# A product of the identity with ones between the down and the up projections of a fp32 feed-forward on Trainium2

## What is computed

```python
FFN_HIDDEN = -(-8 * D_MODEL // (3 * 256)) * 256      # 5632
...
        hf = modulate(rms_norm(x, norm_ffn_gain[l]), sh_f, sc_f)
        gate_h, up_h = jnp.split(hf @ w_ffn_in[l], 2, axis=-1)
        x = x + g_f[:, None, :] * ((jax.nn.silu(gate_h) * up_h) @ w_ffn_out[l])
```

## Time and profile before

| | us |
|---|---|
| median of three runs | 2655.31 (2654.34 to 2657.0) |
| the profiled execution, its own time | 2652.7 |
| its span, first to last instruction | 2650.9 |
| TensorE busy | 2518.7 (95%) |
| GpSimdE busy | 1002.0 (38%) |
| VectorE busy | 912.5 (34%) |
| ScalarE busy | 787.6 (30%) |

### The profile page before, as it was taken

The page is one execution under the profiler, slowest core; times in us unless marked ns, Lnnn a source line. Parts: engine busy times, 40 slices in busy tenths (PEclk is TensorE's granted clock), DMA queues, the critical chain, the costliest instruction groups (busy, mean ns, idle before and its releaser), DMA issues.

```text
span 2650.9 us, 33839 instructions
## 1 busy us (share of the span) xinstructions
PE 2518.7 (95%) x11449; PEld 2036.6 (77%) x11449; DVE 912.5 (34%) x1487; ACT 787.6 (30%) x1490; POOL 1002.0 (38%) x764
## 2 busy tenths in 40 slices
PE   5589999999799999989999999999999999999999
PEld 3577777887677778768888888888888888888887
DVE  4755332157766666675201020202020201010112
ACT  2023224232455542232222222222222222222221
POOL 0024333444200024434444444444444444444443
PEclk8579999999788899989999999999999999999999
DMA  8732122365212246645222222222222222222223
GB/s 307 256 133 80 64 90 88 107 235 192 87 62 68 79 160 223 213 151 183 96 96 95 93 90 94 95 95 95 91 91 95 95 95 94 89 94 95 95 95 111
DMA packets 86204, 315.74 MB, mean 119 GB/s; under 512 B 9584, under 2 KB 10240, under 8 KB 84736
## 3 DMA queue, kind: packets, MB, share of 16 engines
q1 hardware_dynamic: 84240, 303.31, 34.1%
q10 hardware_dynamic: 1904, 11.62, 1.2%
HBM read 310.69 MB, written 4.19 MB: 119 GB/s over the span
## 4 chain that ended last, share of the span: by engine, by line
PE 59%; issue 29%; POOL 10%; DVE 2%; POOLq 0%; ACT 0%; DVEq 0%; ACTq 0%
PE ps L366 55%; POOL wlo L318 10%; PE ps L643 1%; PE ps L672 1%; PE ps L661 1%; DVE macc L1111 1%; PE ps L650 0%; POOLq L317 0%; DVE nsq L1361 0%; DVE biasT L1387 0%; PE ps L678 0%; PE ps L628 0%; POOL kn L340 0%; PE ps L632 0%; DVE rq L1364 0%
## 5 line engine op out<-in xcount | busy, mean ns | idle before, releaser
L318 POOL TENSOR_TENSOR wlo<-raw,whi 128x512 fp32r<-128x512 f32 x728 | 963.5, 1324 | 1481.4 <-ACT whi L800 1222.4
L800 ACT ACTIVATE whi<-raw 128x512 fp32r<-128x512 f32 x612 | 386.5, 632 | 1241.7 <-PE ps L366 1239.1
L366 PE MATMUL ps<-hfH,whi 128*128 128x512 f32 x1408 | 559.3, 397 | 12.3 <-DVE hfL L1493 11.5
L366 PE MATMUL ps<-hfL,whi 128*128 128x512 f32 x1408 | 558.7, 397 | 0.0
L366 PE MATMUL ps<-hfH,wlo 128*128 128x512 f32 x1408 | 558.1, 396 | 0.0
L366 PEld LDWEIGHTS ps<-hfH,whi 128*128 128x128 f32 x1408 | 266.1, 189 | 75.8 <-issue 12.3
L366 PEld LDWEIGHTS ps<-hfH,wlo 128*128 128x128 f32 x1408 | 266.2, 189 | 61.9
L366 PEld LDWEIGHTS ps<-hfL,whi 128*128 128x128 f32 x1408 | 266.2, 189 | 61.0
L1521 DVE SCALAR_TENSOR_TENSOR x1T<-ps,modc,x1T 128x512 f32<-128x512 f32 x176 | 132.1, 750 | 456.2 <-PE ps L366 456.2
L366 PE MATMUL ps<-huH,whi 128*128 128x512 f32 x704 | 279.2, 397 | 0.5 <-DVE huL L1504 0.5
L366 PE MATMUL ps<-huL,whi 128*128 128x512 f32 x704 | 279.1, 396 | 0.0
(11 more groups left out here) (242 smaller groups left out, 2707.0 us busy)
## 6 DMA issues: line engine op xcount, KB each, us to landing
raw<-in_wstream SPq DMA_DIRECT2D x370, 512.0 KB, 3.4
modw<-in_mstream SPq DMA_DIRECT2D x192, 512.0 KB, 4.5
xT<-in_xt SPq DMA_DIRECT2D x4, 1024.0 KB, 8.2
w1s<-in_w ACTq DMA_DIRECT2D x2, 2048.0 KB, 7.9
x1T<-in_xt ACTq DMA_DIRECT2D x4, 1024.0 KB, 8.8
out_y<-x1T SPq DMA_DIRECT2D x16, 256.0 KB, 2.0
cmpb<-in_cmp_tab ACTq DMA_DIRECT2D x1, 1024.0 KB, 5.1
ptab<-in_tabs ACTq DMA_DIRECT2D x1, 768.0 KB, 4.3
```

The source lines that it names most:

```text
L318: nc.gpsimd.tensor_tensor(wlo[:, s, :], raw[:, r, :], whi[:, s, :].bitcast(F32), ALU.subtract).then_inc(unit_ready, 1)
L366: ins = nc.tensor.matmul(acc, lhs, rhs, start=first and n == 0, stop=last and n == 2)
L800: A(whi[:, k % SPLIT, :], raw[:, k % 8, :], ACT.Copy).then_inc(unit_hi, 1)
```

## The change

In each round of the loop TensorE makes one more product, behind the down projection and ahead of the up tile: the identity (held) times ones (moved), 128 x 128 in float32, into the first 128 columns of bank 1. Ahead of it stands a wait for `up_saved` with the value that the up tile behind it waits for as well. Nobody reads the result; the up tile's first pass starts the same bank anew.

```diff
--- before.py
+++ after.py
@@ -780,6 +780,8 @@
                 base = U_FFN + 32 + UNITS_FFN * j
                 gate_tile(base, 4 * j + 4, 0)
                 down_tiles(base + 4, j)
+                pe.wait_ge(up_saved, 4 * j + 3)
+                nc.tensor.matmul(ps[:, 1, 0:P], ident[:, :], ones[:, :], start=True, stop=True)
                 up_tile(base + 20, 4 * j + 4, 0)
                 for p in range(1, 4):
                     gate_tile(base + 24 + 8 * (p - 1), 4 * j + (4 + p), p)
```

## The result

| | before | after |
|---|---|---|
| median, us (6 runs each, same chip) | 2654.8 (2652.5 to 2657.0) | 2641.1 (2637.4 to 2643.6) |
| the profiled execution, its own time | 2652.7 | 2638.3 |
| its span | 2650.9 | 2636.5 |
| from the first huH pass to the end of the span | 1382.1 | 1369.3 |

The ratio of after to before is 0.9945, 95% interval [0.9933, 0.9957]: the changed kernel is faster by 0.4 to 0.7%. The forecast was 2642.3.

A forecast was written before the change was run, and what follows sets the result against it. The prediction took TensorE's matmul count times their spacing as the bound. A price of 2.2 us less a gain of 15.2 gave -13.0 us, from 2655.3 to 2642.3 us, range 2639.8 to 2650.0, chance 0.80.

The forecast's parts named there:

- The bound: Looped part of the feed-forward: time is the count of TensorE matmuls times the spacing of their starts; no other engine counts.
- Two paces for one shape: Loop's hf stretches: the same 384 matmuls run at 228.9 ns each in group 0, 233.3 ns in the others.
- the pace is set elsewhere: Rival, chance 0.07: something not seen at the seam sets the hf spacing; the product only adds its price, 2657.5 us.
- The price: Added product at each seam, two records: 0.22 us each, ten make +2.2 us, bounds 1.2 and 8.6.
- The gain: Hf stretches behind the product: eight groups fall from 89.60 to 87.89 us, the last from 78.39 to 76.91; -15.2 us.
- The mechanism: Seam from down projection to up tile: the slow rhythm is a phase handed over; an fp32 product there breaks it.
- the break is complete with the first: Product at the seam: one record alone costs what each of eight does; argued against the rival that only some groups change.
- nine slow seams: Seams from down projection to up tile: the slow rhythm follows at nine of ten, the fast one at one.
- Only some groups: Rival, chance 0.08: seams differ in phase, so half of the nine groups switch; gain 5.4 us, 2649.9 us.
- A worse rhythm: Rival, chance 0.05: up tiles keep the down projection's 234.3 ns behind the product; +7.7 us, 2663.0 us.

The follow-up runs named there:

- the single product: Kernel before with the fp32 product in round 0 only, that round written out ahead of the loop, none in rounds 1 to 9: 2655.1 us, loop 1382.3.
- the fp32r product: Changed kernel with one fp32r product of 128 held by 128 moved columns (one record) in place of the fp32 product: 2636.7 us, loop 1368.1.
- the transpose: Changed kernel with one fp32 transpose of the identity (one record) in place of the fp32 product: 2640.9 us, ratio to before 0.995, loop 1368.1.

## Why the prediction was right

**The bound.** TensorE alone, no gap in the loop: the chain shows it on both sides. The time is the count of matmuls times their spacing.

**Two paces for one shape.** Right, and both are seen again with the wait alone and with the single product; all other traces have the fast one alone. The wait alone, which also moves the code behind it, leaves 89.60 us, so neither of the two does it. The rival that the pace is set elsewhere and the product is pure cost falls, and with it the rule of the Trainium skill, "TensorE: Matmul & The Clock Gate", section "Back-to-back issue gap", as far as it gives one spacing for a shape. The 216 ns that the prediction took from it is its figure for an isolated gap at 512 columns; for a sustained stream of weight load and matmul the same section has about 131 ns. These traces have neither: they have 228.9, 233.3 and 234.3 ns for 512 columns with one weight load each, at one clock.

**The price.** Taken as 0.22 us from four products in a row; the round of group 0, which was fast before, went from 87.89 to 88.13 us (from the first product's start, 1312.14, to 1400.27): 0.24. Ten make 2.4.

**The gain.** Taken as 15.2 us. Product included, the loop is 12.8 us shorter against 13.0 in the sum. The span fell by 14.4, and the other 1.6 us lie ahead of the first huH pass (1268.78 before, 1267.16 after), where the programs are the same. They belong to the spread.

**The mechanism.** It was right that a phase is handed over from the down projection and that the product acts on it. It was too narrow in one step: "the break is complete with the first" record. The run with the product in round 0 only shows that the phase outlives a product. And a break at the seam isn't needed: with a further full pass a round, or a product ahead of the down projection, all stretches are fast as well. At an unbroken seam it goes by the phase in which the down projection ends: in these traces every stretch behind 231 or 235 is fast, and every one behind 233, 237 or 238 is slow. In the changed kernel that is the same phase in all ten rounds (235 ns would come next), one that goes on fast even at an unbroken seam, as in the run with the product ahead of the down projection. So how much of the changed kernel's gain is the product's stop and how much the phase it leads to can't be parted there. The prediction had nine slow seams, each mended by its own product; in the trace no product stands behind a slow stretch, since the stretch ahead is always fast already, and the forecast came out right without that case being put to the test. That the round with the product keeps coming back to a good phase was not foreseen; as far as the gain rests on it, the number is luck.

**The rivals.** Only some groups: no seam stayed slow with a product in each round, and seven seams at which 233 would have come next are fast behind one record (three with the fp32r product, four with the transpose). The single product shows that the phases do differ from round to round, as this rival supposed. A worse rhythm: no hf stretch reached 234 ns in any run.

**Open.** Why a weight load and a matmul of fixed shapes settle into periods of one, two, three or seven, and what apart from the 32 bytes separates the hu tiles (233.3 ns when shifted) from the hf tiles (228.9 ns in the same shape). No other place for huH was tried, nor hf tiles that are as fresh as hu tiles. And whether a product frees a stretch at a seam behind a slow one (237 or 238 next), eight of the nine cases that the prediction counted on, no run shows.

## What to carry to other kernels

Where TensorE is the bound and has no gaps, compare the spacing of the starts between stretches that run the same instructions; a difference of 2% doesn't show in busy time or waits, but in the duration of single matmuls (397 against 388 to 394 ns here) and in windows with a count. Before adding work to change such a rhythm, look at where the moved tiles start in SBUF: here a shift of 32 bytes gave more than the product and cost nothing. And a product that sets a phase holds only for the sequence it was measured in; any change in the count of matmuls per round has to be looked at again.

## What the runs showed that I had not expected

One more pass of 512 columns a round, pure extra work of 10 x 0.23 us, makes the kernel 12.8 us faster in the loop (1382.1 to 1369.3). Tiles that start 32 bytes past a multiple of 64 were moved at 234.3 ns a matmul, at a multiple of 64 at 233.3, and others of the same shape at 228.9. And a stretch that has fallen into the slow rhythm stayed in it for nine rounds in a row, some 1200 us, in each of three kernels (before, the wait alone, the single product).
